# The first MLP's fourth down group as seven block products, with scaling at the up projection's eviction

## The chip, the cores and the metric

The kernel runs on one core of a Trainium2 chip. The metric is the device time of one execution in microseconds (us). TensorE is called PE, VectorE DVE, ScalarE ACT, GpSimd POOL, and SP is the engine whose queue issues the weight loads.

## The reference, cut to what matters

Three layers run one after the other on 512 tokens of 1024 features in float32: retention with an MLP, chunk attention with an MLP, and a hybrid layer. The change is about the two MLPs and what follows the first of them:

```python
def _rmsnorm(x, g):
    xf = x.astype(jnp.float32)
    y = xf * lax.rsqrt(jnp.mean(xf * xf, axis=-1, keepdims=True) + EPS)
    return (y * g.astype(jnp.float32)).astype(x.dtype)

def _sqrelu_mlp(h, w1, w2):          # w1: 1024 x 4096, w2: 4096 x 1024
    u = jax.nn.relu(h @ w1)
    return (u * u) @ w2

h = h + _sqrelu_mlp(_rmsnorm(h, mlp_norm_g[i]), mlp_w1[i], mlp_w2[i])
```

After the first MLP the next norm (mix_norm_g[1]) and the attention's projection of q, k and v follow.

## The kernel before, in words

**Data.** `h` holds the residual, transposed: 8 tiles of 128 features x 512 tokens. Every float32 operand of a matmul is split in two parts: a high part (ACT copies to fp32r) and a low part (DVE subtracts the high part from the value). A product takes three matmuls: high x high, low x high, high x low (`mm3`, L606 to L608). The norm's gain is applied when `x_hi` and `x_lo` are made from `h`; the factor 1/rms of a token (`rbc`, the same in all partitions) only after the matmul.

**Weights.** SP loads them in units of 128 x 1024 into a ring of four (`raw`). ACT makes `w_hi` (L1248), DVE `w_lo` (L1851); a "split" is this pair. Splits are issued three units ahead. An MLP has 64 units: in each of four groups 8 for 1024 columns of w1 (up) and 8 for 1024 rows of w2 (down).

**Up group.** 8 tiles, each 24 matmuls of 512 columns (`proj`), into two PSUM banks in turn: PE may start tile t + 2 when tile t has been read (`tile_read`). In `mlp_up` ACT reads a tile with Relu (L1459) and squares it (L1463) into `uf`; `rbc` isn't applied. From each pair of tiles sums and differences of the two token halves are made (T1 to T4; B11, B21, B22 are halves themselves), and split by ACT (L1426) and DVE (L2123). In the last three tiles DVE also forms block sums of the down weights (L2141 to L2148: s1, s2, s3, s4) and both engines split the first blocks (L1432, L2128).

**Down group as a seven.** `down_seven` multiplies in Winograd's form, four times over: 7 products of 12 matmuls with 256 columns (`product`, L829) instead of 8. Each product is added by DVE into half-tiles of 256 tokens (`add`, L2204), into `down_sum`, eight tiles that POOL clears at the start of an MLP (L2866). Some products go on in a bank that `add` has to read first: the fourth product (T2, bank 4) waits for the first add. The DVE's order is written out by hand.

**Down group plain.** The last group of each MLP: ordinary up, then 8 tiles of 24 matmuls with 512 columns. Here DVE scales by `rbc` (`scaled`, L1904), and squares with the maximum; POOL multiplies `down_sum` by rbc squared (L2868, L2876), and DVE adds it to `h` (L2322).

**Order of an MLP.** Up, then twice (seven, up) in a loop, a third seven, a plain up group, a plain down group. The loop is on PE, ACT and DVE. As `last_tiles` reads each tile of the last down group, DVE adds it to `h` (L1909), ACT makes `x_hi` (L1255) and the square `sq` (L1263), DVE `x_lo` (L1857), and POOL sums the squares into `acc` (`sum_squares`, L2802, L2806). In the next layer's first tile PE makes the mean square from `acc` (`mean_square`, L686, a hook before the eighth of its k) and in the second the spread of 1/rms over the partitions (`spread_rms`, a hook before the fifth).

**Where the rest stands.** `down_seven` on PE, ACT and DVE; `mlp_up` on ACT and DVE; `mlp` on all four engines; `units` packs the weights on the host.

## Time and profile before

| | |
|---|---|
| time, median of 3 runs | 2090.84 us (2090.55 to 2091.3) |
| profiled execution: span | 2087.9 us |
| profiled execution: its own time beside the span | not on the page; only the span is |
| PE busy | 2077.0 us, 99% |
| DVE, ACT, POOL busy | 1370.3, 989.9, 300.8 us |
| granted TensorE clock | full in every stretch |

Times in the profile count from the span's start. The first MLP runs from about 412 to 752 us, the second from about 992 to 1333. In the page a matmul's duration is longer than the distance to the next one, since they are pipelined: the time that a group of matmuls takes is read from the stretch from the first of them to the first of the next group.

### The profile page before, as it was taken

The page shows a single profiled execution, that of the slowest core. Times are in us where ns is not written, and L with a number is a line of the kernel's source. Part 1 is how long each engine was busy: PE and PEld are TensorE (multiplying, and loading weights), DVE is VectorE, ACT ScalarE, POOL GpSimd, SP SyncE. Part 2 cuts the span into 40 slices and gives each one's busy share as a digit, 9 for nine tenths or more (in the row PEclk, how much of TensorE's full clock was granted, in tenths as well). Part 3 has the DMA queues.
Part 4 walks back from the last instruction along what each step waited for, and adds up shares of the span by engine and source line. Part 5 has one row for each costly group of instructions (what it writes and reads, how often), then busy time and mean ns, then how long its engine had stood idle before and what let it go on. Part 6 is the DMA issues. An engine that isn't in the chain of part 4 may idle for free.

```text
span 2087.9 us, 30411 instructions
## 1 busy us (share of the span) xinstructions
PE 2077.0 (99%) x10596; PEld 1771.9 (85%) x10596; DVE 1370.3 (66%) x2322; ACT 989.9 (47%) x1687; POOL 300.8 (14%) x323
## 2 busy tenths in 40 slices
PE   9999999999999999999999999999999999999998
PEld 8888888889989888888899898878888888888887
DVE  6554544676868654887778687567765456666674
ACT  5433333564553334886645543457652244433343
POOL 2113121300002111443100012312300020000000
PEclk9999999999999999999999999999999999999999
DMA  5232222224324332222232232221222223333222
GB/s 200 83 101 66 100 68 99 82 87 141 99 97 147 101 111 91 76 91 76 71 131 82 100 120 93 97 91 54 82 79 100 100 91 106 108 101 119 100 91 81
DMA packets 58182, 204.31 MB, mean 98 GB/s; under 512 B 6953, under 2 KB 8121, under 8 KB 58080
## 3 DMA queue, kind: packets, MB, share of 16 engines
q1 hardware_dynamic: 53504, 189.29, 27.2%
q0 software_dynamic: 3856, 12.47, 2.0%
q8 instruction: 64, 1.05, 0.2%
q10 hardware_dynamic: 720, 1.18, 0.2%
q14 instruction: 38, 0.31, 0.0%
HBM read 200.79 MB, written 6.06 MB: 99 GB/s over the span
## 4 chain that ended last, share of the span: by engine, by line
PE 96%; ACT 2%; DVE 1%; issue 0%; POOL 0%; ACTq 0%; DVEq 0%
PE bank L606 30%; PE bank L608 30%; PE bank L607 30%; PE bank L928 1%; PE bank L907 1%; PE bank L943 1%; ACT arena L1536 1%; PE bank L941 1%; PE bank L908 1%; PE bank L645 1%; PE bank L818 0%; ACT arena_r L1555 0%; ACT w_hi L1248 0%; ACT arena_r L1544 0%; PE bank L686 0%
## 5 line engine op out<-in xcount | busy, mean ns | idle before, releaser
L606 PE MATMUL bank<-x_hi,w_hi 128*128 128x512 f32 x1552 | 608.3, 392 | 0.0
L607 PE MATMUL bank<-x_lo,w_hi 128*128 128x512 f32 x1560 | 607.3, 389 | 0.0
L608 PE MATMUL bank<-x_hi,w_lo 128*128 128x512 f32 x1552 | 604.5, 389 | 0.0
L1851 DVE TENSOR_TENSOR w_lo<-raw,w_hi 128x1024 fp32r<-128x1024 f32 x306 | 388.4, 1273 | 191.4 <-ACT w_hi L1248 191.0
L606 PE MATMUL bank<-arena_r,w_hi 128*128 128x256 f32 (+1 forms) x1296 | 430.7, 332 | 1.7 <-DVE h L1909 1.3
L608 PE MATMUL bank<-arena_r,w_lo 128*128 128x256 f32 (+1 forms) x1296 | 429.6, 331 | 0.0
L607 PE MATMUL bank<-arena_r,w_hi 128*128 128x256 f32 (+1 forms) x1280 | 423.3, 331 | 0.0
L1248 ACT ACTIVATE w_hi<-raw 128x1024 fp32r<-128x1024 f32 x306 | 320.1, 1052 | 178.2 <-PE bank L608 176.4
L608 PEld LDWEIGHTS bank<-x_hi,w_lo 128*128 128x128 f32 x1552 | 291.3, 188 | 61.5
L607 PEld LDWEIGHTS bank<-x_lo,w_hi 128*128 128x128 f32 x1560 | 293.0, 188 | 59.3
L606 PEld LDWEIGHTS bank<-x_hi,w_hi 128*128 128x128 f32 x1552 | 291.4, 188 | 59.2 <-issue 0.4
L606 PEld LDWEIGHTS bank<-arena_r,w_hi 128*128 128x128 f32 x1296 | 246.2, 190 | 26.7 <-issue 2.5
L608 PEld LDWEIGHTS bank<-arena_r,w_lo 128*128 128x128 f32 x1296 | 246.2, 190 | 23.3
L607 PEld LDWEIGHTS bank<-arena_r,w_hi 128*128 128x128 f32 x1280 | 243.2, 190 | 22.5
L1909 DVE TENSOR_TENSOR h<-bank,h 128x512 f32<-128x512 f32 x96 | 66.0, 690 | 128.8 <-PE bank L608 128.7
L2891 POOL TENSOR_SCALAR arena<-arena,small 128x256 f32<-128x256 f32 (+3 forms) x128 | 90.9, 724 | 234.8 <-DVE small L2370 189.3
L1904 DVE TENSOR_TENSOR arena<-bank,rbc 128x512 f32<-128x512 f32 x77 | 53.0, 688 | 99.3 <-PE bank L608 99.2
L1432 ACT ACTIVATE w_hi<-raw 128x512 fp32r<-128x512 f32 x96 | 58.8, 624 | 77.3 <-PE bank L608 65.4
L1769 ACT ACTIVATE arena<-arena,colv 128x512 f32<-128x512 f32 x44 | 36.0, 818 | 124.5 <-DVE arena L1904 124.5
L2204 DVE TENSOR_TENSOR arena<-bank,arena 128x256 f32<-128x256 f32 x186 | 76.0, 420 | 23.2 <-PE bank L608 21.8
L606 PE MATMUL bank<-w_hi,x_hi 128*128 128x512 f32 x208 | 81.0, 389 | 0.9 <-ACT arena L1620 0.9
L608 PE MATMUL bank<-w_hi,x_lo 128*128 128x512 f32 x208 | 80.9, 389 | 0.0
(293 smaller groups left out, 2543.5 us busy)
## 6 DMA issues: line engine op xcount, KB each, us to landing
raw<-in_stream SPq DMA_DIRECT2D x354, 512.0 KB, 3.2
arena<-in_rel_pad POOLq DMA_DIRECT2D x16, 256.0 KB, 3.7
bias_strips<-bias_strip_once POOLq DMA_DIRECT2D x12, 320.0 KB, 4.2
h<-in_x_t SPq DMA_DIRECT2D x6, 256.0 KB, 8.3
arena<-in_c_decay POOLq DMA_DIRECT2D x4, 256.0 KB, 3.0
arena<-bias_strips POOLq DMA_DIRECT2D x4, 256.0 KB, 4.6
arena<-bias_strips POOLq DMA_DIRECT2D x8, 128.0 KB, 2.4
out_t<-h SPq DMA_DIRECT2D x4, 256.0 KB, 2.2
```

What stands on the lines that cost most here:

```text
L606: pe.matmul(dst, lh, rh, start=start, stop=False, **kw)
L607: pe.matmul(dst, lh, rl, start=False, stop=False, **kw)
L608: return pe.matmul(dst, ll, rh, start=False, stop=stop, **kw)
L645: m = pe.matmul(banks[4 + t][:, :], xk[:, j, t * P:t * P + P], wk[:, slot, cols_k], start=start, stop=stop)
L1248: act.activation(w_hi[:, u % RING, :], raw[:, u % RING, :], ACT.Copy).then_inc(hi_ready, 1)
L1432: act.activation(block_at(slot)[0], src, ACT.Copy).then_inc(done, 1)
L1769: act.activation(cy[2 * (pair.b % 2) + n], cz[2 * (pair.b % 2) + n][:, 2:S + 2], ACT.Identity, scale=col(k + (C_CW + 2 * 2 * PAIRS)), bias ...
L1851: dve.tensor_tensor(w_lo[:, s, :], raw[:, s, :], f32(w_hi[:, s, :]), ALU.subtract).then_inc(lo_ready, 1)
L1904: return dve.tensor_tensor(dst, banks[(at.t - 1) % 2][:, :], rbc[:, :], ALU.mult)
L1909: dve.tensor_tensor(h[:, j, :], banks[(at.t - 1) % 2][:, :], h[:, j, :], ALU.add).then_inc(tile_read, 1)
L2204: dve.tensor_tensor(part, banks[bank][:, 0:QUARTER], part, ALU.add).then_inc(quarter_read, 1)
L2891: pool.tensor_scalar(pf[par][:, a:a + w], pf[par][:, a:a + w], rinv[par][:, t:t + 1], 1.0, ALU.mult, ALU.mult).then_inc(sm.probs, 1)
```

## The change: what it does

The first MLP runs up, then three times (seven, up), then a fourth seven; its plain groups are gone (`SEVENS = [4, 3]`). The second MLP keeps three sevens and the plain last groups. In both, DVE reads each up tile with one instruction, max(tile, 0) x rbc, into `zf`, and ACT squares that, so the sums of the down products need no factor: `add` adds straight into `h`. POOL's clearing, squaring of rbc and multiplying are gone. In the first MLP's last seven (`into`) ACT and DVE make `x_hi` and `x_lo` of each tile of `h` as soon as its last add is done (`TILE_DONE` counts the adds), and the squares. Attention's first tile runs by passes (all high x high, then low parts of the weights with high parts of the input, then the other way round), so that it needs the low parts later; mean square and spread move to later hooks.

```diff
+TILE_DONE = [5, 10, 12, 17, 19, 24, 28, 31]
+SEVENS = [4, 3]
...
-        down_sum = [f_at(9 + j) for j in range(KT)]
... PE
+            def by_passes(count):
+                slot = at.u % RING
+                bank = banks[at.t % 2][:, :]
+                wait(pe, hi_ready, at.u + 1)
+                wait(pe, tile_read, at.t - 1)
+                for k in range(KT):
+                    wait(pe, xh_ready, count + k + 1)
+                    pe.matmul(bank, w_at(slot, k * P, k * P + P)[0], xs(k)[0], start=k == 0, stop=False)
+                wait(pe, lo_ready, at.u + 1)
+                for k in range(KT):
+                    pe.matmul(bank, w_at(slot, k * P, k * P + P)[1], xs(k)[0], start=False, stop=False)
+                for k in range(KT):
+                    wait(pe, xl_ready, count + k + 1)
+                    m = pe.matmul(bank, w_at(slot, k * P, k * P + P)[0], xs(k)[1], start=False, stop=k == KT - 1)
+                m.then_inc(products_done, 1)
+                at.step()
...
-                with pe.Fori(0, 2) as i:
+                with pe.Fori(0, 3) as i:
...
-            proj(first=[(xl_ready, 16)], hooks={7: lambda: mean_square(2)})
-            proj(hooks={4: lambda: spread_rms(2)})
+            by_passes(16)
+            proj(hooks={4: lambda: mean_square(2)})
             for c in range(2):
                 for kk in range(4):
-                    token_major(kk, banks_read=(att_v, 0) if c and kk == 0 else None)
+                    token_major(kk, {1: lambda: spread_rms(2)} if kk + c == 0 else {},
+                                banks_read=(att_v, 0) if c and kk == 0 else None)
... ACT, mlp_up
-                    wait(act, products_done, at.pe)
-                    act.activation(zf[j % 2], banks[(at.t - 1) % 2][:, :], ACT.Relu).then_inc(tile_read, 1)
                     wait(act, tile_read, at.t)
... ACT, down_seven
+                    if into:
+                        for j in range(2 * n - 2, 2 * n) if n < 3 else ():
+                            hi_of(j, into, quarter_read, g * 31 + TILE_DONE[j])
                 at.u, at.pe = at.u + 8, at.pe + 28
                 split(0, p + 20)
+                if into:
+                    for j in range(4, 6):
+                        hi_of(j, into, quarter_read, g * 31 + TILE_DONE[j])
                 split(1, p + 23)
+                if into:
+                    for j in range(3):
+                        square_only(2, j, lo_ready, u + 7)
+                    hi_of(6, into, quarter_read, g * 31 + TILE_DONE[6])
                 split(2, p + 27)
+                if into:
+                    hi_of(7, into, quarter_read, g * 31 + TILE_DONE[7])
+                    for j in range(3, KT):
+                        square_only(2, j, quarter_read, g * 31 + TILE_DONE[j])
... DVE, mlp_up (and the plain up group)
+            def rectify(j):
+                wait(dve, products_done, at.pe)
+                dve.scalar_tensor_tensor(zf[j % 2], banks[(at.t - 1) % 2][:, :], 0.0, rbc[:, :],
+                                         ALU.max, ALU.mult).then_inc(tile_read, 1)
...
                     at.step()
+                    rectify(j)
... DVE, down_seven
-                    part = down_sum[j][:, half * QUARTER:(half + 1) * QUARTER]
+                    part = h[:, j, half * QUARTER:(half + 1) * QUARTER]
...
+                low(0, 1)
                 s3(3)
...
                 a22(3)
+                low(2)
                 add(5, 6, 1, 25)
                 add(5, 7, 0, 25)
                 add(5, 7, 1, 25, 22)
                 at.u, at.pe = at.u + 8, at.pe + 28
+                if into:
+                    add(6, 6, 1, 26, 25)
+                    split(0)
+                    low(3)
+                    add(4, 7, 1, 27, 27)
+                    add(4, 7, 0, 27, 26)
+                    low(4)
+                    add(7, 7, 0, 28, 30)
+                    low(5, 6, 7)
+                    split(1)
+                    split(2)
+                    return
... DVE, plain up group of the second MLP
-                    scaled(zf[j % 2]).then_inc(tile_read, 1)
+                    rectify(j)
                     wait(dve, tile_read, at.t)
-                    dve.scalar_tensor_tensor(uf[j % 2], zf[j % 2], 0.0, zf[j % 2], ALU.max, ALU.mult)\
-                        .then_inc(last_ready, 1)
-                    dve.wait_ge(sums_ready, ready + j + 3)
-                    dve.tensor_tensor(h[:, j, :], down_sum[j], h[:, j, :], ALU.add)
+                    dve.tensor_tensor(uf[j % 2], zf[j % 2], zf[j % 2], ALU.mult).then_inc(last_ready, 1)
... POOL
-                pool.memset(arena[:, 9 * S:17 * S], 0.0).then_inc(sums_ready, 1)
-                pool.tensor_tensor(acc[:, :], rbc[:, :], rbc[:, :], ALU.mult).then_inc(sums_ready, 1)
-                for j in range(KT):
-                    pool.tensor_tensor(down_sum[j], down_sum[j], acc[:, :], ALU.mult).then_inc(sums_ready, 1)
... host
-            if g < 3:
+            if g < SEVENS[n]:
                 rows = rows.reshape(KT // 2, 2, P, D).swapaxes(0, 1).reshape(D, D)
```

`low(j)` makes `x_lo` of tile j (`x_lo_of`) where `into` is given. In `mlp_up` of DVE the eviction stands ahead of all that the tile's turn brings: for an odd tile T1's low part, for the last tile also the block sums s3 and s4 of the second block column, then t2, the low parts of B21 and T2.

## Rows read from the trace of the kernel before

**Rows 1.** The page: busy time and instructions; the chain that ended last by engine.
```profile
PE 2077.0 (99%) x10596; PEld 1771.9 (85%) x10596; DVE 1370.3 (66%) x2322; ACT 989.9 (47%) x1687; POOL 300.8 (14%) x323
...
PE 96%; ACT 2%; DVE 1%; issue 0%; POOL 0%; ACTq 0%; DVEq 0%
```

**Rows 2.** Busy times by stretch, the six sevens: length, engines' busy us, clock, DMA.
```profile
456.65:497.40 40.75, 40.72 (x337) 40.42 (x336) 34.54 (x70) 18.57 (x30) 2.17 (x4) 1.00 0.44 141
...
1037.21:1077.53 40.32, 40.32 (x338) 40.31 (x337) 34.73 (x70) 18.67 (x30) 0.00 (x0) 1.00 0.34 110
...
sum 242.81, PE 242.78 PEld 242.16 DVE 209.30 ACT 112.54 POOL 6.37; mean PE 40.46 PEld 40.36 DVE 34.88 ACT 18.76 POOL 1.06
```

**Rows 3.** Busy times by stretch: a looped up group and the first MLP's plain down.
```profile
581.42:624.97 43.55, 43.55 (x195) 36.04 (x193) 28.37 (x51) 24.46 (x42) 0.00 (x0) 1.00 0.28 92
708.88:752.40 43.52, 43.52 (x193) 36.04 (x192) 19.44 (x24) 16.99 (x23) 9.20 (x6) 1.00 0.29 97
```

**Rows 4.** Timeline of PE, second seven's fourth product: start, us, instruction.
```profile
545.14 0.28 PE L608 MATMUL bank<-arena_r,w_lo 128*128 128x256 f32 x1
545.33 0.39 PE L606 MATMUL bank<-arena_r,w_hi 128*128 128x256 f32 x1
545.55 0.28 PE L607 MATMUL bank<-arena_r,w_hi 128*128 128x256 f32 x1
```

**Rows 5.** Timeline of DVE around the second seven's start; in brackets idle time before.
```profile
540.89 0.69 DVE L2146 TENSOR_TENSOR raw<-raw 128x512 f32<-128x512 f32 x1
541.49 0.69 DVE L2148 TENSOR_TENSOR sq<-raw,sq 128x512 f32<-128x512 f32 x1
542.61 0.43 DVE L2181 TENSOR_TENSOR arena<-arena 128x256 f32<-128x256 f32 x1 [0.43 <-ACT arena L1463]
543.19 1.03 DVE L2123 TENSOR_TENSOR arena_r<-arena,arena_r 128x512 fp32r<-128x512 f32 x2
544.25 0.69 DVE L2128 TENSOR_TENSOR w_lo<-arena,w_hi 128x512 fp32r<-128x512 f32 x1
544.86 1.12 DVE L2204 TENSOR_TENSOR arena<-bank,arena 128x256 f32<-128x256 f32 x3
```

**Rows 6.** Timeline of ACT in the same stretch.
```profile
541.15 0.60 ACT L1459 ACTIVATE arena<-bank 128x512 f32<-128x512 f32 x1 [2.22 <-PE bank L608]
541.86 0.64 ACT L1463 ACTIVATE arena<-arena 128x512 f32<-128x512 f32 x1
542.52 0.97 ACT L1426 ACTIVATE arena_r<-arena 128x512 fp32r<-128x512 f32 x2
543.58 0.64 ACT L1432 ACTIVATE w_hi<-arena 128x512 fp32r<-128x512 f32 x1
```

**Rows 7.** Groups of instructions by form: busy us, mean ns of one, idle before.
```profile
L1255 ACT ACTIVATE x_hi<-h,colv 128x512 fp32r<-128x512 f32 x40 | 29.0, 724 | 70.4 <-DVE h L1909 68.2 <-DMA h<-in_x_t 2.0
L2377 DVE SCALAR_TENSOR_TENSOR arena<-bank,rbc 128x512 f32<-128x512 f32 x29 | 19.8, 683 | 9.8 <-PE bank L608 7.3 <-ACT rbc L1288 2.3
```

**Rows 8.** Timeline of DVE at the end of the third seven.
```profile
660.50 0.69 DVE L2128 TENSOR_TENSOR w_lo<-raw,w_hi 128x512 fp32r<-128x512 f32 x1 [0.30 <-ACT w_hi L1432]
661.21 1.09 DVE L2204 TENSOR_TENSOR arena<-bank,arena 128x256 f32<-128x256 f32 x3
662.22 1.22 DVE L1851 TENSOR_TENSOR w_lo<-raw,w_hi 128x1024 fp32r<-128x1024 f32 x1
```

**Rows 9.** Timeline of POOL ahead of the first MLP: sums of squares.
```profile
397.95 1.29 POOL L2802 TENSOR_TENSOR acc<-sq 128x512 f32<-128x512 f32 x1 [24.22 <-ACT sq L1263]
400.37 1.77 POOL L2806 TENSOR_TENSOR acc<-acc,sq 128x512 f32<-128x512 f32 x1 [1.12 <-ACT sq L1263]
```

**Rows 10.** Timeline of DVE in the same stretch.
```profile
398.86 1.47 DVE L1851 TENSOR_TENSOR w_lo<-raw,w_hi 128x1024 fp32r<-128x1024 f32 x1
400.25 0.74 DVE L1857 SCALAR_TENSOR_TENSOR x_lo<-h,colv,x_hi 128x512 fp32r<-128x512 f32 x1
...
401.58 1.12 DVE L1857 SCALAR_TENSOR_TENSOR x_lo<-h,colv,x_hi 128x512 fp32r<-128x512 f32 x1
```

More of the change, by code:

```diff
@@ L870, in down_seven, with mlp @@
                 at.u = at.u + 8
-            def mlp(q, n, g):
+            def mlp(q, n, g, sevens):
                 proj(first=[(xl_ready, 8 * q)], hooks={7: lambda: mean_square(n)})
@@ L882, in mlp @@
                         proj()
-                    at.leave(2)
-                down_seven(Lin(g + 2))
-                for _ in range(8):
-                    proj()
-                proj(lambda k: (uh[k], ul[k]), first=[(last_lo, g // 3 * 8)])
-                for _ in range(7):
-                    proj(lambda k: (uh[k], ul[k]))
-            mlp(1, 1, 0)
+                    at.leave(3)
+                if sevens == 4:
+                    down_seven(Lin(g + 3))
+                else:
+                    proj(lambda k: (uh[k], ul[k]), first=[(last_lo, 0)])
+                    for _ in range(7):
+                        proj(lambda k: (uh[k], ul[k]))
+            mlp(1, 1, 0, SEVENS[0])
             def scores(sm, hd, half, kind):
@@ L1468, in mlp_up, with down_seven @@
                         combo_his(kk, T2, 1, combo_sum, sums + (4 * kk + 2))
-            def down_seven(g):
+            def down_seven(g, into=None):
                 u, p, sums = at.u, at.pe, g * 16
@@ L1511, in mlp @@
                 mlp_up(Lin(g))
+                if sevens == 4:
+                    with act.Fori(0, 3) as i:
+                        at.enter(i, 16, 36, 8)
+                        down_seven(Lin(g, 1, i))
+                        mlp_up(Lin(g + 1, 1, i))
+                        at.leave(3)
+                    down_seven(Lin(g + 3), into)
+                    return
                 with act.Fori(0, 2) as i:
@@ L1520, in mlp @@
                     at.step()
[L1521 removed]
+                    wait(act, last_ready, j + 1)
                     act.activation(uh[j], uf[j % 2], ACT.Copy).then_inc(last_hi, 1)
[L1524 to L1525 removed]
+            mlp(1, 0, SEVENS[0], C_MIX1)
             def exps(sm, hd, par, window=False):
@@ L2190, in mlp_up, with down_seven, low @@
                         block_sums(g, 1, u + 2, True)
-            def down_seven(g):
+            def down_seven(g, into=None):
                 u, p, made, rd = at.u, at.pe, g * 20, g * 31
+                def low(*js):
+                    for j in js if into else ():
+                        x_lo_of(2, j, into)
                 def add(bank, j, half, done, behind=None):
@@ L2300, in down_seven, with mlp @@
                 split(2)
-            def mlp(n, g):
+            def mlp(n, g, sevens, into=None):
                 rms(n)
                 dve.wait_ge(rbc_ready, n + 1)
-                ready = g // 3 * 10
-                dve.wait_ge(sums_ready, ready + 1)
                 mlp_up(Lin(g))
+                if sevens == 4:
+                    with dve.Fori(0, 3) as i:
+                        at.enter(i, 16, 36, 8)
+                        down_seven(Lin(g, 1, i))
+                        mlp_up(Lin(g + 1, 1, i))
+                        at.leave(3)
+                    down_seven(Lin(g + 3), into)
+                    return
                 with dve.Fori(0, 2) as i:
```

31 lines of the change are left out of this document (10 added, 21 removed).

## The prediction

> **What bounds the kernel now.** I read the page first: TensorE (PE) is busy 99% of the span and the chain that ended last is 96% PE [rows 1]. So the time is PE's work plus the places where PE waits, and an edit elsewhere counts only through such a place. Next the busy times by stretch. A down group as seven block products ("a seven") takes 40.32 us where PE never waits [rows 2]: 336 matmuls of 256 columns, 0.120 each. A plain down group takes 43.52 us for 192 matmuls of 512 columns, 0.227 each [rows 3]. The six sevens take 242.81 us in all, so they lose 242.81 - 6 x 40.32 = 0.89 us to waits [rows 2]. VectorE (DVE) is busy 28.37 of 43.55 us in a looped up group [rows 3], and 209.30 of 242.81 us in the sevens [rows 2]: there it has little room. Last I read the instructions around the start of a seven [rows 4 to 6] and around its end [rows 8].
>
> The profiled span is 2087.9 us; the page gives no longer time for that execution. The median of the runs is 2090.84, so 2.94 us lie around the span, and I add them unchanged.
>
> **The PE work.** The first MLP's fourth down group goes from 43.52 to 40.32 us: -3.20. The pass-wise first tile of attention has the same 24 matmuls of 512 columns, and the mean square and the spread are moved, not added. This is all that PE gains, beside what is left of the 0.89.
>
> **Scaling at the eviction, inside an up group.** Each of 8 tiles gets one DVE eviction (PSUM times rbc, 0.68 us by a line of the same kind [rows 7]); ScalarE (ACT) loses its Relu, 0.60 [rows 6]. DVE rises to 28.4 + 8 x 0.69 = 33.9 of 43.55 us. The two banks rotate and a tile takes 43.55/8 = 5.4 us, so an eviction a microsecond late hides behind the next tile. Behind the waiting eviction stand DVE's low parts and sums; they catch up before the next tile. I cost it at 0; without that cover each late tile would cost its lateness. At 0 too: the memset, the square of rbc and the multiplications that GpSimd (POOL) loses, and the additions into h of the second MLP's last up (none of them releases PE); the adds into h instead of down_sum (same shape); the weights' new order (same eight units; SP's waits on lo_ready shift with their releasers); ACT's extra high parts inside the last seven, where ACT is busy 18.8 of 40.4 us on average [rows 2].
>
> **The start of each seven.** Here I expect the loss. Look at the second one, S = 540.95. The last up tile is out of PE at 541.15 (Relu starts, S + 0.20). While ACT does Relu and Square, DVE does the two block sums (541.49 is the second) and idles 0.43 until t2 at 542.61; then come the low parts of B21 and T2, the low part of s4 (544.25) and the first add (544.86, ends 545.28) [rows 5, 6]. PE's fourth product adds into bank 4, which that add must have read. It was due at S + 36 x 0.120 = 545.27 and starts at 545.33; the two gaps there are 0.19 and 0.22 instead of 0.12: 0.17 lost [rows 4]. So this place has no slack today.
>
> After the change DVE is held at the eviction until 541.15, and T1's low part and both sums queue behind it. Starts follow each other by 0.60 us for 512 columns (540.89 to 541.49 [rows 5]) and 0.34 for 256 (three adds in 1.09, one 0.42 [rows 8]). Eviction S + 0.20, T1 low S + 0.80, sums S + 1.14 and S + 1.74, t2 S + 2.34 instead of S + 1.66. Square is done by S + 1.6 and no longer decides. T2's high part on ACT starts at S + 2.9 and takes 0.4; s4's high part follows, S + 3.3 to 3.97 (0.64 [rows 6]); its low part S + 4.0; the first add S + 4.61 to 5.03; PE goes on at S + 5.08, not S + 4.32: 0.76, with the 0.10 that the second gap shows as the price of a restart, 0.86. From below the price is 0, from above 1.3, if T1 and both sums (0.34 + 0.60 + 0.60, less the idle 0.43) fell on the path with no cover. I take 0.86 for the five sevens that follow a looped up. The first seven of each MLP follows an up outside the loop; that of the second MLP loses nothing today [rows 2], so I take 0.65 there. Together 5 x 0.86 + 2 x 0.65 = 5.6. Of today's 0.89 I take 0.46 as lying at this place and leave the first seven's 0.43 (40.75 - 40.32 [rows 2]) as it is: +5.1. PE and DVE are late by about the same, so I expect nothing more inside a seven.
>
> The Trainium skill ("VectorE: DVE Perf Modes", The DRAIN you can't avoid) says that the next vector instruction starts only when the pipe is empty. The rows show starts 0.60 apart for instructions of 0.69 [rows 5], so the measurement decides; by the rule each seven would lose some 0.35 more, 2.5 in all.
>
> **From the first MLP into attention.** T is the end of PE's last product. Before, all but one eighth of the norm's input was ready when the last tile ended; now tiles 4 to 7 of h are finished in the last products, and PE reaches the mean square after 36 matmuls of 512 columns, T + 8.16. DVE's tail by the third seven (T = 665.33): low part of the last block T - 4.83, three adds 1.09, a whole split 1.22 [rows 8]; inserted before the last add are x_lo of tiles 2, 3 and 4 (0.74 each alone [rows 10]), and the adds of products 26 and 27. So tile 7 of h is whole at T + 1.5, or T + 1.95 with POOL in the way. ACT's x_hi of tile 7 (0.72 [rows 7]) ends at T + 2.7, and PE's first pass wants it at T + 1.59: a first wait of 1.1.
>
> Then the sums of squares, which were spread over eight tiles, come in a row. POOL's add takes 1.29 where it starts first, but 1.77 where it starts inside an x_lo: it ends 1.15 after the x_lo ends (402.14 against 400.99). DVE's split that starts inside an add takes 1.47, the x_lo 1.12 instead of 0.74 [rows 9, 10]. I read that as taking turns: an x_lo and an add make 1.15 + 0.74 - 0.19 = 1.7, a split and an add 1.15 + 1.22 - 0.13 = 2.24 (0.19 and 0.13 is how early DVE starts before POOL's end, by its length alone). From T + 2.6 there are three x_lo, two splits and five adds: 3 x 1.7 + 2 x 2.24 = 9.6, so the mean square can start at T + 12.3 instead of T + 8.16. PE meets this lateness in pieces (x_hi of tile 7, x_lo of tile 7, the second weight tile, the mean square) that add up to 4.1; with restarts +4.3. From below, with no turns, squares from T + 2.6 and five adds at 1.35 give T + 9.8: 1.6. From above, if DVE's instructions all go first or three splits fall in between: 6. I take 4.3, nearest to the rows. The root, the diagonal and the spread then have 24 matmuls, 5.4 us, before PE wants them: 0.
>
> **Sum.** -3.2 + 5.1 + 4.3 = +6.2: a span of 2094.1, a time of 2097.0.
>
> **Rivals.** (1) Bank 4 comes free in time. If the first add ends by S + 4.3 in the new order too, for which speaks that DVE has 0.43 us idle there and against which that the two sums alone fill three times that, the sevens cost nothing: -3.2 - 0.46 + 4.3 = +0.6, 2091.5. It decides once the chain is 0.7 us shorter than I reckon; at 0.3 shorter the sum is still +4. Not slower. (2) No turns at the transition: DVE and POOL overlap, 1.6 instead of 4.3: +3.5, 2094.3. For it: the add at 397.95 took its 1.29 with a split of DVE's beginning inside it; against: that split's 1.47 and the two instructions after it [rows 9, 10]. (3) The delay spreads: DVE, at 86% in the sevens, doesn't recover beside PE, and every seven loses again what the first loses today, 7 x 0.43 = 3.0: 2100.0. For it the 86%; against, that five of six sevens lose under 0.2 today. That the change doesn't do its work on PE at all I can't see: the fourth group's matmuls are counted.
>
> **How the numbers follow.** What a measurement here can tell from no change is 0.2%, 4.2 us. Forecast 0.50, rival 1 0.14, rival 2 0.22, rival 3 0.14. Forecast and rival 3 are slower, less 0.05 for a forecast that comes out under +4.2; rivals 1 and 2 are within, less 0.03 for both together with a shorter tail than I can see. Faster by 4.2 would need more than the 3.2 + 0.89 that PE can give at all. So faster 0.03, same 0.38, slower 0.59. The range leaves out the lower half of rival 1 and what lies beyond rival 3: 2091.0 to 2100.5; the forecast's own is 2095 to 2099.
>
> **What would show it.** Right: the fourth seven about 40.3 plus its wait; in every seven a gap at the fourth product of 0.6 to 0.9, ended by DVE's first add; two to four gaps after the first MLP, the last before the mean square, ended by POOL. Wrong: no gap at the fourth product (rival 1), POOL's five adds at 1.3 (rival 2), new gaps later in the sevens (rival 3), or PE waiting for evictions inside an up group, which I cost at nothing.

## The result, and the profile after

| | before | after |
|---|---|---|
| time, median of 5 runs each on one chip | 2090.55 us (2089.76 to 2091.3) | 2097.7 us (2097.0 to 2097.83) |
| profiled span | 2087.9 us | 2095.4 us |

The changed kernel is slower: ratio 1.0035 [1.0024, 1.0045], +7.15 us; the spans differ by 7.46. All ratios here leave out one execution of experiment 11, 10454.81 us at a mean granted clock of 0.186. The page of after, busy times and chain, against [rows 1]: PE has 0.8 us less to do, DVE 41 us more, and the chain that ended last holds more of DVE.

```profile
PE 2076.2 (99%) x10740; PEld 1776.2 (85%) x10740; DVE 1411.1 (67%) x2433; ACT 977.8 (47%) x1679; POOL 263.6 (13%) x303
...
PE 95%; ACT 2%; DVE 2%; issue 1%; POOL 0%; DMA 0%; ACTq 0%; DVEq 0%; POOLq 0%
```

Next the same stretches as in [rows 2], now seven of them: busy times by stretch of after (length; then PE, PEld, DVE, ACT, POOL; granted clock; DMA share and GB/s).

```profile
457.07:498.01 40.94, 40.56 (x337) 40.36 (x336) 35.62 (x72) 18.18 (x29) 2.13 (x4) 1.00 0.46 138
541.56:582.71 41.15, 40.57 (x338) 40.36 (x336) 35.77 (x72) 18.29 (x29) 2.10 (x4) 1.00 0.43 135
...
710.92:751.88 40.96, 40.54 (x337) 40.36 (x336) 37.16 (x75) 22.33 (x38) 0.61 (x1) 1.00 0.35 104
...
sum 287.17, PE 283.94 PEld 282.51 DVE 251.68 ACT 131.79 POOL 6.94; mean PE 40.56 PEld 40.36 DVE 35.95 ACT 18.83 POOL 0.99
```

Seven sevens without a wait would take 7 x 40.32 = 282.24 us, so 4.93 are lost, against 0.89 in the six of before: +4.04. The fourth one is there (40.96, of which 0.64 is waiting, instead of the plain 43.52 of [rows 3]): the 3.20 of PE work is real. The loss stands at one place, the fourth product. The timeline of PE in the second seven, beside [rows 4] (start, duration, instruction; idle time and its end in brackets):

```profile
545.75 0.28 PE L608 MATMUL bank<-arena_r,w_lo 128*128 128x256 f32 x1
546.61 0.39 PE L606 MATMUL bank<-arena_r,w_hi 128*128 128x256 f32 x1 [0.58 <-DVE h L2254]
```

0.86 from one matmul to the next, where 0.12 is usual. The timeline of DVE shows why, beside [rows 5]:

```profile
541.76 0.69 DVE L2191 SCALAR_TENSOR_TENSOR arena<-bank,rbc 128x512 f32<-128x512 f32 x1 [0.23 <-PE bank L608]
...
542.70 0.68 DVE L2184 TENSOR_TENSOR raw<-raw 128x512 f32<-128x512 f32 x1
543.30 0.69 DVE L2186 TENSOR_TENSOR sq<-raw,sq 128x512 f32<-128x512 f32 x1
543.91 0.42 DVE L2226 TENSOR_TENSOR arena<-arena 128x256 f32<-128x256 f32 x1
...
545.53 0.69 DVE L2166 TENSOR_TENSOR w_lo<-arena,w_hi 128x512 fp32r<-128x512 f32 x1 [0.27 <-ACT w_hi L1451]
546.14 1.07 DVE L2254 TENSOR_TENSOR h<-bank,h 128x256 f32<-128x256 f32 x3
```

Counted from the seven's start (541.56) the eviction begins at 0.20, the sums at 1.14 and 1.74, t2 at 2.35, s4's low part at 3.97, the first add at 4.58. Before, that add began at 544.86 - 540.95 = 3.91.

The rest is at the passage into attention, where nothing waited before. The timeline of PE after the first MLP (T = 751.88):

```profile
754.37 0.50 PE L624 MATMUL bank<-x_hi,w_hi 128*128 128x512 f32 x1 [0.71 <-ACT x_hi L1274]
...
759.58 0.50 PE L606 MATMUL bank<-x_hi,w_hi 128*128 128x512 f32 x1 [1.06 <-DVE w_lo L1889]
...
765.15 1.05 PE L704 MATMUL bank<-ones,acc 128*128 128x1 f32 x8 [2.56 <-POOL acc L2872]
766.07 0.75 PE L606 MATMUL bank<-x_hi,w_hi 128*128 128x512 f32 x1
766.62 0.63 PE L607 MATMUL bank<-x_lo,w_hi 128*128 128x512 f32 x1
767.04 0.63 PE L608 MATMUL bank<-x_hi,w_lo 128*128 128x512 f32 x1
```

Three waits: for `x_hi` of tile 7, for the second weight tile's low part (with `x_lo` of tile 7 ahead of it on DVE), for the sums of squares. Behind them the matmuls are 0.43 apart instead of 0.23. The table by stretch names it: the granted clock (third number from the right) is 0.53 in these 3.6 us.

```profile
758.50:765.90 7.40, 3.79 (x20) 2.92 (x19) 5.48 (x3) 0.19 (x1) 7.22 (x5) 1.00 0.56 151
765.90:769.50 3.60, 3.60 (x11) 2.93 (x11) 1.86 (x6) 0.20 (x1) 0.26 (x1) 0.53 0.75 258
769.50:775.00 5.50, 5.50 (x25) 4.48 (x25) 0.47 (x1) 1.11 (x2) 0.91 (x2) 1.00 0.03 12
```

And what made the third wait, POOL's adds and DVE's instructions beside them, against [rows 9, 10]. POOL:

```profile
754.98 10.12 POOL L2872 TENSOR_TENSOR acc<-acc,sq 128x512 f32<-128x512 f32 x5 [0.62 <-ACT sq L1292]
```

DVE:

```profile
753.15 0.41 DVE L2254 TENSOR_TENSOR h<-bank,h 128x256 f32<-128x256 f32 x1
753.49 3.80 DVE L1895 SCALAR_TENSOR_TENSOR x_lo<-h,colv,x_hi 128x512 fp32r<-128x512 f32 x3
757.21 6.77 DVE L1889 TENSOR_TENSOR w_lo<-raw,w_hi 128x1024 fp32r<-128x1024 f32 x3
```

2.02 for an add that takes 1.29 where it starts first [rows 9], 2.26 for a split that takes 1.22 [rows 8].

**Where the 7.46 us are.** By distances between the same marks of both traces: up to the first seven +0.42; first MLP -0.93 (-3.20, +2.27 at the starts of its four sevens); passage, from there to the next common wait of PE (787.55 in the trace before), +6.78; attention -0.12; second MLP +1.78, the starts of its three; the rest of the kernel -0.45. What stands in the first MLP, the passage and the second MLP is read from single profiles to a tenth, the whole from medians.

The rest of the kernel, which no edit touches, needs one more look. It lasts 841.85 to 842.4 us in six of the thirteen profiles (before, after, experiments 2, 5, 9 and 10) and 843.3 to 843.5 in the seven others: there the granted clock falls once more, shortly after a later mean square. The same place in experiments 1 and 10:

```profile
1344.00:1347.40 3.40, 3.40 (x10) 2.62 (x9) 1.88 (x7) 0.21 (x1) 0.00 (x0) 0.50 0.71 270
1342.10:1345.50 3.40, 3.40 (x17) 2.75 (x16) 1.74 (x6) 0.21 (x1) 0.00 (x0) 1.00 0.67 263
```

Ten matmuls instead of seventeen in the same 3.40 us. PE's work ahead of it is the same in both, and no edit touches it, so this fall is none of their doing that can be seen; it adds 1.5 us to the profiles that have it, and two spans can't be compared without looking for it.

### The profile page after: what moved, and what is told of

Its sections match the earlier page's. It is cut to its first block, busy times and chain, and to the rows that moved or that the text cites. A ratio compares the mean times of both kernels' runs of the same rounds, so it can differ in the third digit from the quotient of the medians.

```text
span 2095.4 us, 31083 instructions
## 1 busy us (share of the span) xinstructions
PE 2076.2 (99%) x10740; PEld 1776.2 (85%) x10740; DVE 1411.1 (67%) x2433; ACT 977.8 (47%) x1679; POOL 263.6 (13%) x303
## 3 DMA queue, kind: packets, MB, share of 16 engines
q10 hardware_dynamic: 720, 1.18, 0.2%
## 4 chain that ended last, share of the span: by engine, by line
PE 95%; ACT 2%; DVE 2%; issue 1%; POOL 0%; DMA 0%; ACTq 0%; DVEq 0%; POOLq 0%
PE bank L606 30%; PE bank L608 30%; PE bank L607 29%; PE bank L946 1%; PE bank L925 1%; PE bank L961 1%; PE bank L959 1%; PE bank L926 1%; PE bank L663 1%; ACT arena L1574 1%; POOL acc L2872 0%; ACT arena_r L1593 0%; DMA h<-in_x_t 0%; PE bank L704 0%; DVE w_lo L1889 0%
## 5 line engine op out<-in xcount | busy, mean ns | idle before, releaser
L1889 DVE TENSOR_TENSOR w_lo<-raw,w_hi 128x1024 fp32r<-128x1024 f32 x298 | 376.9, 1269 | 187.0 <-ACT w_hi L1267 186.7
L606 PE MATMUL bank<-arena_r,w_hi 128*128 128x256 f32 (+1 forms) x1344 | 437.7, 326 | 4.9 <-DVE h L2254 2.8
L608 PE MATMUL bank<-arena_r,w_lo 128*128 128x256 f32 (+1 forms) x1344 | 436.4, 325 | 0.0
L607 PE MATMUL bank<-arena_r,w_hi 128*128 128x256 f32 (+1 forms) x1328 | 430.2, 324 | 0.0
L1267 ACT ACTIVATE w_hi<-raw 128x1024 fp32r<-128x1024 f32 x298 | 311.3, 1051 | 173.7 <-PE bank L608 171.3
L606 PEld LDWEIGHTS bank<-arena_r,w_hi 128*128 128x128 f32 x1344 | 255.7, 190 | 28.3 <-DVE h L2254 4.0
L608 PEld LDWEIGHTS bank<-arena_r,w_lo 128*128 128x128 f32 x1344 | 255.7, 190 | 20.7
L607 PEld LDWEIGHTS bank<-arena_r,w_hi 128*128 128x128 f32 x1328 | 252.7, 190 | 20.1
L1451 ACT ACTIVATE w_hi<-raw 128x512 fp32r<-128x512 f32 x112 | 68.5, 623 | 90.0 <-PE bank L608 76.2
L2254 DVE TENSOR_TENSOR h<-bank,h 128x256 f32<-128x256 f32 x217 | 87.4, 416 | 25.7 <-PE bank L608 24.1
L1942 DVE TENSOR_TENSOR arena<-bank,rbc 128x512 f32<-128x512 f32 x61 | 42.0, 688 | 88.0 <-PE bank L608 88.0
L1480 ACT ACTIVATE arena<-arena 128x512 f32<-128x512 f32 x56 | 35.4, 632 | 135.6 <-DVE arena L2191 132.3
```

Source lines behind the costliest of these rows:

```text
L606: pe.matmul(dst, lh, rh, start=start, stop=False, **kw)
L607: pe.matmul(dst, lh, rl, start=False, stop=False, **kw)
L608: return pe.matmul(dst, ll, rh, start=False, stop=stop, **kw)
L1267: act.activation(w_hi[:, u % RING, :], raw[:, u % RING, :], ACT.Copy).then_inc(hi_ready, 1)
L1451: act.activation(block_at(slot)[0], src, ACT.Copy).then_inc(done, 1)
L1480: act.activation(uf[j % 2], zf[j % 2], ACT.Square).then_inc(u_ready, 1)
```

## The experiments

"Transition" is the passage as just marked: 35.15 us before, 41.93 after. Ratios are to the kernel before, run beside it on the same chip. Theory: the change loses at two separate places, DVE's order at a seven's start, and DVE and POOL taking turns at the passage.

**1. Scaling at the eviction without the fourth seven** (scale_only). The first MLP keeps its plain last group, the mean square its place.

```diff
-SEVENS = [4, 3]
+SEVENS = [3, 3]
...
-            mlp(1, 0, SEVENS[0], C_MIX1)
+            mlp(1, 0, SEVENS[0])
+            last_tiles(2, 2, C_MIX1, 1)
...
```

> One part of the change alone: scaling at the up tile's eviction and adds straight into h in both MLPs, but the first MLP keeps three sevens and its plain last groups, and attention starts as before the change. Theory: six sevens with a gap of 0.64 to 0.84 at the fourth product, so 6 x 0.73 = 4.4 against the 0.9 that the sevens lost before: +3.5, a time near 2094.1. Rival (the loss lies in the fourth seven and the passage into attention alone): no change, 2090.6.

Measured 2094.06, ratio 1.0019 [1.0010, 1.0029]; transition 35.15, as before. The last line of the table of its six sevens:

```profile
sum 246.01, PE 243.37 PEld 242.14 DVE 214.70 ACT 109.35 POOL 6.35; mean PE 40.56 PEld 40.36 DVE 35.78 ACT 18.22 POOL 1.06
```

246.01 - 242.81 [rows 2] = 3.20 more, with none of the passage's loss. The two places are separate. (That this equals the 3.20 of PE work is chance.)

**2. POOL's sums cut to 16 columns** (narrow_sums). The mean square of that norm leaves out nearly all tokens.

```diff
+                wide = 16 if n == 2 else S
...
-                pool.tensor_tensor(acc[:, :], sq[:, 0, :], sq[:, 1, :], ALU.add).then_inc(acc_sum, 1)
+                pool.tensor_tensor(acc[:, 0:wide], sq[:, 0, 0:wide], sq[:, 1, 0:wide], ALU.add).then_inc(acc_sum, 1)
...
```

> The changed kernel with POOL's seven sums of squares ahead of attention cut from 512 columns to 16, with the same waits and counts; the mean square of that norm is thus left out for most tokens. Theory of turns: with no long adds of POOL's, x_lo takes 0.74 and a split 1.22 everywhere after the first MLP; the wait for x_hi of tile 7 falls from 0.98 to about 0.5, the wait for the second weight tile (1.33) and the one before the mean square (2.7, with 1.9 of slow matmuls after it) vanish: 2091.3. Rival (DVE's and ACT's orders are late by themselves): the first two waits stay at 2.3 in all and only the mean square's goes: 2093.0.

Measured 2092.29, ratio 1.0009 [1.0000, 1.0019]; transition 35.83. DVE's timeline:

```profile
753.06 2.07 DVE L1895 SCALAR_TENSOR_TENSOR x_lo<-h,colv,x_hi 128x512 fp32r<-128x512 f32 x3
755.04 2.35 DVE L1889 TENSOR_TENSOR w_lo<-raw,w_hi 128x1024 fp32r<-128x1024 f32 x2
```

The same three `x_lo` in 2.07 instead of 3.80, a split in 1.18 instead of 2.26, and 6.10 of the 6.78 are gone: POOL's wide adds were the cause of the waits (one of 0.3 for `x_hi` is left), and DVE's instructions had been slow because of them. The Trainium skill ("SBUF — State Buffer", Who interferes with whom) says that a DVE instruction with two SBUF inputs contends with a GpSimd instruction that reads SBUF, and that the ports they share are an exclusive lock; these rows agree: 3.80 for three `x_lo` beside the wide adds, 2.07 beside the narrow ones.

**3. The first squares earlier** (early_squares): ACT squares tiles 0 to 3 inside the last seven, 4 and 5 before the second split.

```diff
+                    if into and n == 3:
+                        for j in range(4):
+                            square_only(2, j, lo_ready, u + 7)
...
+                    for j in range(4, 6):
+                        square_only(2, j, quarter_read, g * 31 + TILE_DONE[j])
```

> The changed kernel with one order turned: in the fourth seven ACT squares tiles 0 to 3 of h ahead of the last block's high part and tiles 4 and 5 right after their x_hi, so that POOL's sums start some 9 us earlier. Theory (sums of squares and DVE's x_lo and splits take turns, and too many come at once): the 2.7 us before the mean square go, the slow matmuls behind it (PE clock 0.51) go with them, 1.9 us, and of the 2.3 us before that about half; 2092.5. Rival (the tail is bound by the last adds and DVE's own order, the squares only come last): the mean square still waits, by 1 to 2 us, since the last sums depend on tile 7 alone: 2095.5.

Measured 2096.29, ratio 1.0030 [1.0018, 1.0043]; transition 38.74. A miss. PE's waits in 740 to 780:

```profile
PE bank L624 <- ACT x_hi L1274: 2.7, 1, 2.7
PE bank L704 <- POOL acc L2875: 0.3, 1, 0.3
```

The mean square is nearly in time, but the first wait has grown from 0.71 to 2.7. DVE's timeline has the reason:

```profile
748.45 1.77 DVE L2169 TENSOR_TENSOR w_lo<-raw,w_hi 128x512 fp32r<-128x512 f32 x1 [0.30 <-ACT w_hi L1451]
...
753.55 1.77 DVE L1898 SCALAR_TENSOR_TENSOR x_lo<-h,colv,x_hi 128x512 fp32r<-128x512 f32 x1
```

The earlier adds now block what leads to the last add into `h`. Moving the adds moves the turns; it doesn't remove them.

**4. T1's low part and the block sums ahead of the last eviction** (sums_first).

```diff
                     at.step()
+                    if j == 7:
+                        combo_los(g, kk, T1, 1, 2)
+                        block_sums(g, 1, u + 2, False)
                     rectify(j)
...
```

> The changed kernel with one order turned: for the last tile of an up group DVE makes T1's low part and the second block column's two sums ahead of the eviction, not behind it. Theory (the eviction holds DVE, and 1.5 us of ready work queues behind it on the way to the first add, which frees bank 4): the gap at the fourth product of each seven, 0.64 to 0.84 us in the changed kernel, falls to 0.2 or less; seven times 0.6 gives 4 us, a time near 2093.5. Rival (DVE is simply too full with eight more evictions per up group, in whatever order): the gaps stay or move to a later product, and the time stays near 2097.5. The gaps after the first MLP stay in either case.

Measured 2104.0, ratio 1.0066 [1.0049, 1.0083]. A miss by 10 us, in the wrong direction. DVE's timeline at the second seven, whose start is 541.69:

```profile
541.59 0.42 DVE L2161 TENSOR_TENSOR arena_r<-arena,arena_r 128x256 fp32r<-128x256 f32 x1
...
543.13 0.68 DVE L2191 SCALAR_TENSOR_TENSOR arena<-bank,rbc 128x512 f32<-128x512 f32 x1
544.68 0.43 DVE L2228 TENSOR_TENSOR arena<-arena 128x256 f32<-128x256 f32 x1 [0.86 <-ACT arena L1480]
```

DVE, still busy with the blocks' low parts, comes to T1's only as the seven starts, so the 1.5 us of work ahead of the eviction hold the eviction itself (1.44 after the start instead of 0.20), and DVE then idles 0.86 for ACT's square. The sevens take 291.15 together, 3.98 more than in after; the other 3 us of this profile go with the clock, 1.5 in the passage (43.47, with the clock at 0.50 for 6.7 us instead of 0.53 for 3.6) and 1.5 in the untouched rest. Work can only move ahead of the eviction if DVE has the time for it there.

**5. The first add ahead of s4's low part** (add_first).

```diff
-                s4(0)
                 add(4, 0, 0, 1)
+                s4(0)
```

> The changed kernel with one pair of DVE instructions turned: at the start of a seven the first add stands ahead of the low part of s4, which has waited for ACT (0.27 us idle in the changed kernel's second seven). Theory (PE's fourth product waits for nothing but that add's read of bank 4): the add ends some 0.6 to 0.9 earlier, the gap at the fourth product (0.64 to 0.84 in each of seven sevens, 4.94 in all) goes to 0.2 or less, and the time falls by 4 to 5: 2093. Rival (PE waits there for what stands before the add too, T2's low part or the block's): the gap shrinks by 0.3 at most, and the time by 2.

Measured 2095.73, ratio 1.0027 [1.0016, 1.0038]. The table of the second MLP's three sevens:

```profile
1042.34:1082.65 40.31, 40.31 (x337) 40.31 (x336) 35.48 (x72) 18.07 (x29) 0.00 (x0) 1.00 0.36 108
...
```

With one line moved the wait is gone; those three sevens have no loss left at all (120.97 together, against 123.00 in after). In the first MLP's first seven another wait came up. DVE's timeline there:

```profile
469.94 0.69 DVE L2283 TENSOR_TENSOR arena<-raw 128x512 f32<-128x512 f32 x1 [1.64 <-DMA raw<-in_stream]
```

DVE waits for a weight transfer and PE for DVE: that seven takes 41.64. The kernel before has this wait too, 1.02 of DVE's time and about 0.4 of PE's: it is the first seven's 0.43 that I left standing. In after PE doesn't wait there, since it is late already. The profile's span is 3.1 us below that of after, but the median only 2.0, not the 4 to 5 expected: this profile is the fastest of eight executions (2093.95 to 2097.40), whose mean granted clock falls from 0.999 in the fastest to 0.997 in the slowest.

**6. The block sums later** (sums_late): out of `mlp_up`, to behind T3's low part in the seven.

```diff
-                        if j == 7:
-                            block_sums(g, 1, u + 2, False)
...
                 combo_los(g, 3, T3, 2, 5)
+                block_sums(g, 1, u + 2, False)
```

> The changed kernel with the second block column's last two sums put off from the last up tile into the seven, behind the low part of the last T3. Theory (the two sums, 1.2 us, are what the eviction pushed onto the way to the first add): t2 follows Square at once, the add is 0.6 to 0.7 earlier, the gap at the fourth product goes to 0.2 or less: 2093.5. Rival (DVE has no room: at 86% busy in a seven, work put off there comes back as a wait): gaps of the same sum appear at later products of the seven, where there are none now, and the time stays near 2097.5.

Measured 2097.76, ratio 1.0038 [1.0024, 1.0052]. The rival was right in the main: the gap at the fourth product goes, and gaps come back at later ones. The sevens gain 1.3 (285.89 against 287.17), and the clock's fall in the untouched rest takes 1.5 in this profile. The second seven, PE's timeline:

```profile
559.35 0.28 PE L608 MATMUL bank<-arena_r,w_lo 128*128 128x256 f32 x1
559.66 0.39 PE L606 MATMUL bank<-arena_r,w_hi 128*128 128x256 f32 x1
```

There DVE has run without a pause since 548.5, and an add ends at 559.61. DVE has no room for 1.2 us more in that stretch; the sevens take 40.77 to 40.89.

**7. Mean square and spread 1.5 weight tiles later, two more splits ahead of them** (late_hooks).

```diff
-            proj(hooks={4: lambda: mean_square(2)})
+            proj()
...
-                    token_major(kk, {1: lambda: spread_rms(2)} if kk + c == 0 else {},
+                    token_major(kk, {} if c or kk > 1 else {1: lambda: (mean_square, spread_rms)[kk](2)},
...
```

> The changed kernel with the mean square one and a half weight tiles of attention later (inside the first token-major unit) and the spread inside the second; the two splits that would queue behind the root on ACT and DVE are made ahead of it. POOL's sums, DVE's and ACT's orders before that stay. Theory: the sums end some 13 us after the first MLP as now, but PE has other work until then: the wait of 2.7 before the mean square goes, and the slow matmuls after it (granted clock 0.51 to 0.55) with it, since PE no longer stands still; the waits of 0.98 and 1.33 stay. 6.8 too long becomes some 2: 2093. Rival (the clock fell for the sum of the waits and not for the last one): slow matmuls still follow, after the 1.33, and some 1.5 of the 4.9 stay: 2094.5.

Measured 2094.16, ratio 1.0017 [1.0008, 1.0027]; transition 37.53, so 4.40 less than after. The table by stretch where after had its third wait and the low clock:

```profile
760.00:770.00 10.00, 10.00 (x50) 8.39 (x49) 8.27 (x8) 1.27 (x2) 5.99 (x5) 1.00 0.76 221
```

Neither is left. The first two waits stay (0.71 and 1.04), and after those two alone the clock stays at 1.00.

**8. Late hooks, and the last seven's order** (tail2): squares of tiles 0 to 3 in the seven, the others behind all `x_hi`; on DVE `low(4)` behind the last add.

```diff
...
-                    low(4)
                     add(7, 7, 0, 28, 30)
-                    low(5, 6, 7)
+                    low(4, 5, 6, 7)
```

> As late_hooks, and the order around the end of the fourth seven spread: ACT squares tiles 0 to 3 early and 4 to 7 last, makes x_hi of tiles 6 and 7 ahead of the third split; DVE makes the last add ahead of x_lo of tile 4. Theory of turns: fewer of POOL's adds meet DVE's x_lo and splits in the last 6 us, so x_hi of tile 7 is there when PE wants it (a wait of 0.3 or less for 0.98) and the second weight tile too (0.3 or less for 1.33): the passage is at most 1 us longer than before the change, against 6.8: 2091.5. Rival (the early sums only move the turns ahead, as in the kernel with early squares, where x_hi of tile 7 waited 2.9): the first wait grows to 2 or more: 2093.5.

Measured 2092.78, ratio 1.0011 [1.0001, 1.0020]; transition 36.23. The second wait is gone, the first stays (0.75), and the fourth seven takes 41.31, since two `x_lo` and a low part met POOL's early adds. DVE's timeline:

```profile
742.31 3.32 DVE L1899 SCALAR_TENSOR_TENSOR x_lo<-h,colv,x_hi 128x512 fp32r<-128x512 f32 x2
745.55 1.78 DVE L2173 TENSOR_TENSOR w_lo<-raw,w_hi 128x512 fp32r<-128x512 f32 x1
```

**9. Both cures together** (mended): 5 and 8, and s3's low part ahead of `low(0, 1)`, `low(3)` behind the last add.

```diff
...
-                low(0, 1)
                 s3(3)
                 add(6, 7, 1, 22)
                 add(7, 6, 0, 23, 20)
+                low(0, 1)
...
                     split(0)
-                    low(3)
                     add(4, 7, 1, 27, 27)
                     add(4, 7, 0, 27, 26)
-                    low(4)
                     add(7, 7, 0, 28, 30)
-                    low(5, 6, 7)
+                    low(3, 4, 5, 6, 7)
```

> The changed kernel with the three mends together: the first add of a seven ahead of s4's low part on DVE; the mean square and the spread later; and in the first MLP's last seven the squares of tiles 0 to 3 early, DVE's low part of s3 and its adds of products 22 and 23 ahead of x_lo of tiles 0 and 1, and x_lo of tiles 3 to 7 behind the last add into h (both new). Theory (the loss is those two places and nothing else): the first MLP has the length it had with the first add moved, 293.8 us, or 292.0 if the wait for a transfer in its first seven (0.94 in that run) and the restarts behind it don't come again; the transition 35.5 (36.23 with the last mend, less 0.66 for one x_lo that no longer stands ahead of the last add; 35.15 in the kernel before); the second MLP 208.1. Against the kernel before that is -2.0 to -3.8, +0.4 and -0.2 us: 1.8 to 3.6 us faster, ratio 0.998 to 0.999. Rival (what the mends save comes back elsewhere, since DVE and POOL have no room in the last seven): the moved x_lo and the sums of squares hold back the low parts of the last seven or the first passes of attention, the transition stays over 37 us or the fourth seven over 41 us, and the kernel is at 2090.5 to 2092, no faster than before.

Measured 2090.87 against 2090.83, ratio 1.0000 [0.9991, 1.0009]. The fourth seven is at 40.31, the first wait at 0.38 with its restart, but a new wait of 1.79 stands before the second weight tile: transition 37.55, as the rival had it. First, where the first seven lost 0.95 again, the chain of waits (start, length, what):

```profile
463.82 5.68 DMA raw<-in_stream
```

Then DVE's timeline before the new wait:

```profile
754.24 1.79 DVE L1899 SCALAR_TENSOR_TENSOR x_lo<-h,colv,x_hi 128x512 fp32r<-128x512 f32 x1
755.95 2.30 DVE L1893 TENSOR_TENSOR w_lo<-raw,w_hi 128x1024 fp32r<-128x1024 f32 x1
```

**10. Experiment 1 with the add moved** (scale_add_first).

> The kernel that has the scaling at the eviction alone (six sevens, the first MLP's last down group plain, the mean square where it was), with the first add of a seven ahead of s4's low part. Theory (scaling at the eviction costs only the wait at the fourth product, and the add's place in DVE's order is what causes it): each of the six sevens falls from 40.94 to 41.14 us back to 40.31 to 40.35, 0.62 to 0.79 each, together 4.1 us less than the kernel without the move: 2090.0 us, no difference from the kernel before, and the gain of the seventh seven is then all that the whole change has to give. Rival (s4's low part, half a microsecond later, is needed by a product soon after, or the first seven waits for its transfer as it did in the earlier run): a gap of 0.3 or more in every seven, or 0.9 in the first, and the kernel stays at 2091 or above.

Measured 2091.18 against 2090.83, ratio 1.0002 [0.9993, 1.0011]. The last line of the table of its six sevens:

```profile
sum 243.57, PE 243.17 PEld 242.23 DVE 213.00 ACT 108.47 POOL 6.35; mean PE 40.53 PEld 40.37 DVE 35.50 ACT 18.08 POOL 1.06
```

So moving one add gives back 2.44 of the 3.20 that scaling at the eviction cost in experiment 1, and not the 4.1 expected. In the second MLP the theory holds: its sevens are back at 40.32 to 40.37. In the first MLP 0.83, 0.46 and 0.31 are left, the first with a wait for its transfer (PE 0.45), as the rival had it, and the time is the rival's. The two profiles' spans differ by 3.7, but 1.6 of that lies in the untouched rest, where experiment 1 has the clock's fall.

**11. Mended, the last four squares later** (squares_later). The edit is shown against experiment 9.

```diff
...
                 split(2, p + 27)
-                if into:
-                    for j in range(4, KT):
-                        square_only(2, j, quarter_read, g * 31 + TILE_DONE[j])
...
                     split()
                     if n == 2:
+                        for j in range(4, KT):
+                            square_only(2, j, quarter_read, (SEVENS[0] - 1) * 31 + TILE_DONE[j])
                         split(4, at.pe + 1)
```

> The kernel with the three mends (first add ahead, later mean square, reordered last seven), and the squares of tiles 4 to 7 on ACT behind the split of the fourth weight tile instead of ahead of it, so that POOL's last four adds begin some 3 us later (757 instead of 754.05) and no longer beside DVE's x_lo of tiles 6 and 7 and its split of the second weight tile. Theory (the 1.79 wait at 756.29 in that kernel is those three DVE instructions taking turns with POOL's adds; the mean square, wanted at 766.6 and summed up at 761.6, has 5 us to spare): five x_lo in a row take 3.4 instead of 4.44, the split 1.2 instead of about 2.2, the wait goes, and the transition falls from 37.55 to 35.7 us; everything else stays, so the span is 2085.8 to 2086.0 and the time about 1.8 below that kernel's, 2089.0, ratio to the kernel before 0.999. Rival (the adds only meet the next splits instead, or the mean square comes late): a wait of the same size at the third or fourth weight tile or before the mean square, transition 37 us or more, no gain.

Measured 2090.63 against 2090.55, ratio 0.9998 [0.9989, 1.0008], which just holds the 0.999 that was expected; transition 36.71, not 35.7. The wait of 1.79 went, as the theory had it. DVE's timeline:

```profile
751.48 3.40 DVE L1898 SCALAR_TENSOR_TENSOR x_lo<-h,colv,x_hi 128x512 fp32r<-128x512 f32 x5
754.79 4.63 DVE L1892 TENSOR_TENSOR w_lo<-raw,w_hi 128x1024 fp32r<-128x1024 f32 x4
```

A wait of 1.04 before the mean square took its place, the rival's. POOL's four adds, by source line (shortest, median, longest ns):

```profile
L2876 POOL TENSOR_TENSOR acc<-acc,sq x4: 1288/1722/5679, 754.9 to 763.4; 128x512 f32<-128x512 f32 x4
```

This time DVE kept its pace, four splits at 1.22 each one behind the other, and one add stood for 5.68 us. No version beats the kernel before by what can be measured here.

## Why the prediction was right, step by step

The time was 2097.7, forecast 2097.0 and slower. Both places of loss and what waits there were forecast. Of the three terms one was exact and two were off in opposite directions, by -1.1 and +2.5: that the total came within about a microsecond is in part luck.

- **PE work, -3.2.** Right: the fourth group is a seven, 40.96 with its wait.
- **Start of each seven, +5.1: measured +4.04.** The mechanism is the one that was forecast, in its order and nearly to the hundredth: eviction 0.20 after the start as reckoned, sums 1.14 and 1.74 as reckoned, first add 4.58 instead of 4.61. That this could be reckoned from starts 0.60 apart bears out the choice against an empty pipe ahead of every instruction, which would have put the add some 0.35 later. The Trainium skill ("VectorE: DVE Perf Modes", The DRAIN you can't avoid) has that as its rule, but adds what the prediction left out: an instruction that isn't held starts earlier; these starts agree with the addition. The sevens that begin behind a looped up and aren't the last of their MLP lost 0.80 to 0.83, against 0.86; the two last ones 0.64 and 0.62, forecast at 0.86 too, and the first of each MLP 0.62, against 0.65. Of the 1.1 that was forecast too much, 0.46 stands in the two last ones, and ACT's timeline has the reason: T2's high part and s4's, in the second seven and in the fourth.

```profile
544.36 0.42 ACT L1445 ACTIVATE arena_r<-arena 128x256 fp32r<-128x256 f32 x1 [0.50 <-DVE arena L2226]
544.87 0.63 ACT L1451 ACTIVATE w_hi<-arena 128x512 fp32r<-128x512 f32 x1
...
713.72 0.42 ACT L1445 ACTIVATE arena_r<-arena 128x256 fp32r<-128x256 f32 x1 [0.50 <-DVE arena L2226]
714.04 0.61 ACT L1451 ACTIVATE w_hi<-arena 128x512 fp32r<-128x512 f32 x1
```

0.51 from one to the other against 0.32, and only in the former does DVE idle for it (0.27, shown above). In all twelve traces with the change the distance is 0.47 to 0.51 in the sevens that the loop's jump back leads to, and 0.30 to 0.33 in the first of an MLP and behind the loop's end. Experiment 1 has a shorter loop in the first MLP, and there the third seven, now behind the loop's end, takes 40.94 instead of 41.12. So the difference goes with the jump; what holds ACT there isn't shown, and the trace of before has one late start (0.50) behind a loop's end too. The other large part is the 0.43 that I left standing in the first seven: experiment 5 shows it to be a transfer, and a transfer's lateness and DVE's don't add up, they lie side by side.
- **Passage, +4.3: measured +6.78.** `x_hi` of tile 7 was ready at T + 2.5 (forecast 2.7), three waits came in the forecast order, the mean square began at T + 13.27 instead of T + 12.3. That makes 13.27 - 8.16 = 5.1 instead of 4.1; the adds began at T + 3.1 instead of T + 2.6, since ACT's next square comes behind that `x_hi` and takes 0.6 (in the forecast the adds begin before that `x_hi` ends), and took 10.1 instead of 9.6, since three splits met them and not two. (Two sums of the forecast are off by a little: 2.6 + 9.6 is 12.2, not 12.3, and five adds at 1.35 from T + 2.6 end at T + 9.35, not T + 9.8.) The term that was missing is the clock: the eight matmuls after the third wait are 0.43 apart at a granted clock of 0.53, which is the 1.2 GHz level, where 0.23 is the 2.4 GHz level: from 766.07 to 769.57 they take 3.50 instead of 8 x 0.227, with 0.1 for the restart, = 1.9. That is 1.6 more, and 5.1 + 1.6 = 6.7. The fall is there in all four profiles with the three waits (after, experiments 4, 5 and 6) and in none of the nine others at this place; since it also comes and goes elsewhere without a wait, the three waits as its cause are argued, not shown.
- **Evictions inside an up group, at 0.** Right: PE waits at no eviction in the list of its waits, and the up group after the first seven lasts 43.55, as before. The 0.42 ahead of the first seven isn't the change's either: it arises in the first 14 us of the kernel, where PE waits 1.3 for the `x_hi` of its input in this profile; the wait differs between profiles (0.57 in experiment 1), and the first seven begins at 456.65 to 458.46 with it.
- **Rivals.** Bank 4 in time: refuted by every seven's gap. No turns: refuted by the adds at 2.02 and by experiment 2. Delay spreading inside the sevens: not in after, but it is what experiment 6 produced.

Where the gain went: the 3.2 us of PE work are less than either loss. With both cured the kernel is back where it was, and not below it: of the 3.2, 1.0 goes, net of what those of before lost, to the transfer and other small waits in the first MLP's sevens, and 1.6 to 2.4 stay at the passage (36.71 or 37.55 against 35.15). By the stages of its profile experiment 11 would be some 1.0 us below the kernel before (first MLP -2.3, passage +1.6, second MLP -0.25), too little to be seen in a median. In a plain last group the norm's input becomes ready tile by tile, beside PE's work; in the seven, tiles 4 to 7 become ready at its end, and their `x_hi`, `x_lo`, squares and sums must be done while PE is already consuming them.

## What to carry to other kernels

When an instruction that waits for PE is put into a hand-ordered queue, list what stands between it and the next thing PE needs, and move that thing first; here one moved line gave back 2.4 us of the six sevens (246.01 and 243.57, experiments 1 and 10). Before a stage ends in another form, look at what its last outputs feed and how much of that was hidden by their coming one after another. And two engines that take turns make moving work in time a poor cure: of the reorderings at the passage, experiments 3, 8, 9 and 11 each opened a new wait. And before two spans are compared, compare the granted clock of a stretch that neither edit touches: here it was worth 1.5 us.

## What the runs showed of the hardware

- DVE and POOL take turns by whole instructions, and the cost isn't shared evenly: 2.30 for each split and 2.15 for each add between them in strict alternation in one order (experiment 9), four splits at 1.22 and one add at 5.68 in another (experiment 11). What decides which of the two happens isn't settled by these runs.
- The clock fell to the lower level after three waits in a row (0.71, 1.06, 2.56 idle), and stayed at 1.00 after one wait of 2.7 (experiment 3), after 0.71 and 1.04 (experiment 7) and after two of 0.27 and 1.79 (experiment 9). That fall alone was worth 1.6 us. In seven of the thirteen profiles it also fell in the untouched rest, without a wait, at the same work of PE as in the six others (0.50 and 1.00 in the two rows shown): the same work doesn't always get the same clock.
- PE's restart after a wait: the first matmul is followed after 0.22 instead of 0.12 (256 columns) or 0.34 instead of 0.23 (512), after idle times of 0.34 to 2.73 alike (once 0.19 for 256 columns).
- An ACT instruction of the next stage starts 0.47 to 0.51 after the one before it where a loop's jump back lies between them, and 0.30 to 0.33 where the loop is entered or left (all twelve traces with the change).
